# Feed-forward output projections with every matmul split into two 64-row halves

## What is computed

```
def swiglu(h, w_in, w_out):
    g, u = jnp.split(h @ w_in, 2, axis=-1)
    return (jax.nn.silu(g) * u) @ w_out

# in second_block, for each layer
h = modulate(rms_norm(x, norm_g[layer, 0]), sh1, sc1)
x = x + 0.5 * g1[:, None, :] * swiglu(h, ffn_w_in[layer, 0], ffn_w_out[layer, 0])
...
h = modulate(rms_norm(x, norm_g[layer, 2]), sh3, sc3)
x = x + 0.5 * g3[:, None, :] * swiglu(h, ffn_w_in[layer, 1], ffn_w_out[layer, 1])
```

## Time and profile before

| | |
|---|---|
| median of 3 runs | 3966.06 us |
| profiled execution | 3976.6 us, of which the span from first to last instruction is 3974.8 us |
| mean granted TensorE clock | 0.938 |
| PE busy | 3643.8 us, 92% |
| DVE busy | 2207.9 us, 56% |
| ACT busy | 1592.4 us, 40% |
| matmul records | 19924 |

### The profile page before, as it was taken

The page is one execution under the profiler, slowest core; times in us unless marked ns, Lnnn a source line. Parts: engine busy times, 40 slices in busy tenths (PEclk is TensorE's granted clock), DMA queues, the critical chain, the costliest instruction groups (busy, mean ns, idle before and its releaser), DMA issues.

```text
span 3974.8 us, 52209 instructions
## 1 busy us (share of the span) xinstructions
PE 3643.8 (92%) x19924; PEld 2788.9 (70%) x19924; DVE 2207.9 (56%) x3277; ACT 1592.4 (40%) x2692; POOL 303.7 (8%) x401
## 2 busy tenths in 40 slices
PE   8998796998999586998999998999999999889998
PEld 7886475666787454456878766787877878667877
DVE  7866855886874784236772336565233332654332
ACT  3335744887423662113222336322233222453222
POOL 0110001110210002001210000111000001000001
PEclk9999588999999758999999999999999999999999
DMA  7561013997555005997773310575323223302222
GB/s 276 175 172 61 2 59 123 365 362 277 185 191 150 1 33 212 403 395 251 271 251 101 101 64 11 180 232 197 106 82 125 96 96 103 130 33 88 95 93 74
DMA packets 164958, 618.35 MB, mean 156 GB/s; under 512 B 18540, under 2 KB 20117, under 8 KB 163581
## 3 DMA queue, kind: packets, MB, share of 16 engines
q1 hardware_dynamic: 114928, 420.58, 29.7%
q0 software_dynamic: 45568, 166.75, 12.8%
q10 hardware_dynamic: 4238, 27.90, 1.8%
HBM read 595.95 MB, written 16.31 MB: 154 GB/s over the span
## 4 chain that ended last, share of the span: by engine, by line
PE 82%; DVE 8%; ACT 5%; DMA 2%; issue 2%; SPq 0%; ACTq 0%; POOL 0%; DVEq 0%; POOLq 0%; PEldq 0%
PE psum L2500 23%; PE psum L2513 12%; PE psum L838 12%; PE psum L923 5%; PE psum L990 4%; PE psum L2103 4%; PE psum L767 3%; PE psum L2334 3%; PE psum L2122 2%; DMA ring<-wtile 1%; PE psum L2355 1%; PE psum L1207 1%; PE psum L1217 1%; PE psum L775 1%; DVE spare L1313 1%
## 5 line engine op out<-in xcount | busy, mean ns | idle before, releaser
L791 ACT CAST small_r<-ring 128x1024 fp32r<-128x1024 f32 x264 | 276.0, 1048 | 1081.9 <-PE psum L838 336.9
L795 DVE TENSOR_TENSOR ring_r<-ring,small_r 128x1024 fp32r<-128x1024 f32 x264 | 323.7, 1228 | 687.9 <-ACT small_r L791 687.7
L791 ACT CAST PB_r<-ring 128x1024 fp32r<-128x1024 f32 x248 | 257.3, 1049 | 545.8 <-PE psum L2500 327.9
L795 DVE TENSOR_TENSOR ring_r<-ring,PB_r 128x1024 fp32r<-128x1024 f32 x248 | 299.6, 1222 | 247.6 <-ACT PB_r L791 247.2
L2500 PE MATMUL psum<-H_r,ring_r 128*128 128x512 f32 x1344 | 336.1, 392 | 0.0
L2500 PE MATMUL psum<-H_r,small_r 128*128 128x512 f32 x1344 | 326.9, 395 | 0.0
L2500 PE MATMUL psum<-H_r,PB_r 128*128 128x512 f32 x1344 | 318.6, 389 | 0.0
L2500 PEld LDWEIGHTS psum<-H_r,small_r 128*128 128x128 f32 x1344 | 252.3, 188 | 61.2
L2500 PEld LDWEIGHTS psum<-H_r,ring_r 128*128 128x128 f32 x1344 | 252.2, 188 | 56.0
L2500 PEld LDWEIGHTS psum<-H_r,PB_r 128*128 128x128 f32 x1344 | 252.3, 188 | 53.4
L838 PE MATMUL psum<-H_r,small_r 128*128 128x512 f32 (+1 forms) x1040 | 275.4, 368 | 0.0
(11 more groups left out here) (443 smaller groups left out, 6615.5 us busy)
## 6 DMA issues: line engine op xcount, KB each, us to landing
ring<-wtile SPq DMA_DIRECT2D x776, 512.0 KB, 5.1
spare<-wmod POOLq DMA_DIRECT2D x97, 512.0 KB, 4.8
H<-wmod POOLq DMA_DIRECT2D x48, 512.0 KB, 4.6
PB<-wmod POOLq DMA_DIRECT2D x48, 512.0 KB, 4.4
X<-wmod POOLq DMA_DIRECT2D x47, 512.0 KB, 5.1
PB<-wahead POOLq DMA_DIRECT2D x16, 512.0 KB, 7.7
h_rows<-PB POOLq DMA_DIRECT2D x10, 512.0 KB, 4.5
PB<-wmod SPq DMA_DIRECT2D x4, 1024.0 KB, 15.2
```

The source lines that it names most:

```text
L791: nc.scalar.copy(high(j), slot(g0 + j)).then_inc(high_ready.sem, 1)
L795: nc.vector.tensor_tensor(low(g0 + j), slot(g0 + j), high(j).bitcast(F32), ALU.subtract).then_inc(low_ready.sem, 1)
```

## The change

Each matmul of the output phase is made as two. The first contracts partitions 0 to 63 of the weight tile and of the hidden, into bank 4 or 5 as before. The second contracts partitions 64 to 127, into bank 6 or 7. Both have 128 output rows and 512 columns. `out(j)` adds the two banks to `X` one after the other; the second addition waits for the first, since it reads what that wrote.

```
+            ROW_HALVES = (slice(0, P // 2), slice(P // 2, P))
...
-                                    mm = nc.tensor.matmul(bank[4 + j % 2][:, :], w_part[:, k * P:(k + 1) * P], HID2[x][:, kk * NLAT:(kk + 1) * NLAT],
-                                                          start=(not last and kk == 0 and x == 0), stop=(last and kk == FT - 1))
+                                    for h, r in enumerate(ROW_HALVES):
+                                        mm = nc.tensor.matmul(bank[4 + j % 2 + 2 * h][:, :], w_part[r, k * P:(k + 1) * P], HID2[x][r, kk * NLAT:(kk + 1) * NLAT],
+                                                              start=(not last and kk == 0 and x == 0), stop=(last and kk == FT - 1))
...
-                    nc.vector.scalar_tensor_tensor(Xv[:, j, 0:NLAT], bank[4 + j % 2][:, :], coef[:, 16 + j:17 + j], Xv[:, j, 0:NLAT],
+                    V(eng, nc.vector.scalar_tensor_tensor(Xv[:, j, 0:NLAT], bank[4 + j % 2][:, :], coef[:, 16 + j:17 + j], Xv[:, j, 0:NLAT], ALU.mult, ALU.add))
+                    nc.vector.scalar_tensor_tensor(Xv[:, j, 0:NLAT], bank[6 + j % 2][:, :], coef[:, 16 + j:17 + j], Xv[:, j, 0:NLAT],
                                                    ALU.mult, ALU.add).then_inc(dve_freed.sem, 1)
```

## The result

The changed kernel takes 3977.43 us (median of 20 runs, 3963.78 to 3992.29) beside 3964.60 us for the kernel before (20 runs, 3952.99 to 3971.49). The ratio is 1.0028, with a 95% interval of 1.0019 to 1.0037. It is slower by some 11 us (0.0028 x 3965), more than the 4.8 us forecast, inside the stated range and beyond the 0.2% that the prediction took as the limit of no change, though the interval just reaches down to it. The mean granted clock over the 20 runs of the changed kernel is 0.9380.

The account below looks back on a forecast made before the run. TensorE was taken as the bound, with 82% of the chain of waits. 1.6 us of offsets and 3.2 us of additions, with nothing for the clock, made +4.8 us on 3966.06, about 3971 us; range 3952 to 3990.

Parts of the forecast that it names:

- The likeliest case: Whole kernel: pairs as fast as single matmuls, 3958 to 3974 us, no change beyond 7.9 us; chance 0.50.
- a cost kept by each pair: Output-phase matmuls: each pair costs 1.5 to 12 ns more than a whole matmul, so slower; chance 0.28.
- Pairs run together: Output phase on TensorE: two 64-row matmuls run at the same time, taking as long as one 128-row matmul.
- 1.6 us for an offset once per wait: Output phase: 7 to 10 ns at each of 192 waits, two per weight tile, +1.6 us.
- The bounds of -30 and +21 us: Output-phase pairs: limits from halves winning 14 ns per pair to an extra 10 ns per pair.
- 3.2 us for four additions on the chain: End of each output phase: the last tile's second addition adds 0.79 us, four times, +3.2 us; the 28 others hidden.
- Nothing for the clock, with 5 us either way: After the longer idle behind three phases: granted clock loss taken as unchanged, bounded by 3 x 1.7 = 5 us.
- The first rival: Output-phase matmuls: each pair keeps a cost, 7 ns or 14.8 us, giving 3984 us; chance 0.28 for 1.5 to 12 ns.
- the second, faster halves: Output-phase matmuls: halves escape a slowdown in reading by 8 ns, 17 us less, giving 3954 us; chance 0.08.
- Serial halves: Output-phase matmuls: fp32r halves do not overlap, 0.230 us each, +486 us, 4455 us; chance 0.08.
- Exposed loads: Output phase: each weight load waits for the matmul before it on the same rows, +397 us, 4366 us; chance 0.06.

Follow-up runs that it names:

- same_rows: The changed kernel with both matmuls of a pair on rows 0 to 63, same counts, banks and additions: 5297.76 us.
- halves_only: The changed kernel's half matmuls in two banks, but one addition, of the first bank only: 3962.35 us, 1.0001 of the kernel before.
- again: The changed kernel run once more, unaltered: 3974.11 us, 1.0019 of the kernel before.
- adds_only: The kernel before with whole matmuls, but each addition doubled, the same bank added twice at half the scale: 3974.13 us, 1.0020 of the kernel before.
- one_half: The changed kernel with only the first half of each matmul, rows 0 to 63, and one addition: 4378.23 us.
- last_whole: The changed kernel with the last output tile of each feed-forward in whole matmuls and one addition: 3970.68 us, 1.0018 of the kernel before.
- four_adds: The kernel before with whole matmuls, but four chained additions of the same bank at a quarter of the scale: 3985.9 us, 1.0058 of the kernel before.
- the filled kernels: The kernel before and the changed one, each with three unused matmuls in the wait after the first three feed-forwards: 3960.7 us (0.9989) and 3961.3 us (0.9999).

## Why the prediction was right, and where it was off

The forecast was 3971 us and the time 3977.4, in the range of 3952 to 3990. The likeliest case, no change beyond 7.9 us, did not come by the ratio of 1.0028, which lies just outside it, on the side that had 0.42. That side was meant for a cost kept by each pair, which is not there, so that the time came slower and inside the range is in part luck: the room made for such a cost took in a loss of clock that was put at nothing.

- **Pairs run together.** Right, and shown by `same_rows` and `halves_only`. The row that carried it was the fp32 score product, four records in 1.13 us beside two in 1.12; it held for fp32r in a stream of 2112 pairs.
- **1.6 us for an offset once per wait.** Too much: the steady 24 pairs take 5.59 us in both traces, and `halves_only` has 492.2 us of phases as before. The starts of a pair were to be a few ns apart; they are 3 to 37 ns apart, and it costs nothing. The bounds of -30 and +21 us were not needed. The first rival, a cost of each pair, is refuted at this pace, and so is the second, faster halves.
- **3.2 us for four additions on the chain.** Right in each place: 6.09 to 6.88 us at three and 2.43 to 3.21 at the last. In the traces the 28 others hold nothing up.
- **Nothing for the clock, with 5 us either way.** This is the mis-sized term. The runs put 6 to 7 us on it, by a mean clock of 0.9385 in place of 0.9409, all of it a loss and beyond the bound of 5, and it comes with the additions and not with the halves. The prediction counted the stretch right behind the idle, where the first pairs of `again` and `adds_only` are no longer than those of profiles with the short wait. How the remaining microseconds spread over later stretches was not found; one profile per kernel is too few, since stages that are not changed differ by as much from profile to profile (from the end of the third first pair to the fourth input phase before took 211.4 us and `halves_only` 206.4).
- **The rivals' prices.** Serial halves were priced at +486 us, at the full clock. The run that made them serial lost 1308 us in the phases, at a granted clock of 0.50. Exposed loads did not come; the trace of `one_half` has them covered on the same rows.

Still open: the 5.6 us of `last_whole`, which stretches hold the loss of clock, and with it whether the added idle causes that loss or only goes with it. For a cause speak `four_adds` and the filled kernels, against it the table of waits and `last_whole`.

## What to carry to other kernels

Two matmuls on different row halves, into different banks and near each other in the queue, take the time of one, so a split by contraction rows neither costs nor gains on TensorE; what it costs is the second bank's addition where that stands behind the last matmul. Do not price such a step by its length on the chain alone: here 3.2 us on the chain came to about 10. Where TensorE waits for a chain of other engines, a few matmuls without use can keep the clock: with three of them the first pair took 7.49 us at all six places, 1.6 less than the usual 9.05. The gain for the whole kernel, 4 us by the means, is not clear of the noise.

## What the runs showed of the hardware

- A stream of fp32r matmuls of rows 0 to 63 alone ran at a granted clock of 0.50 with PE busy all the time, 0.426 us for 512 columns; two such streams on different rows ran at 1.00, 0.230 us a pair. Half the array in use took nearly twice the time of all of it.
- Matmuls on free rows start ahead of earlier ones that wait for theirs, over a limited reach: 175.4 us a phase where full overlap gives 122.9.
- Four matmuls of 32 rows and their four loads fit in 0.230 us.
- The loss of clock behind an idle TensorE was 1.6 us of a first pair of 9.05 (7.49 where it was filled, and once without); from profile to profile the same wait of 6.09 us was followed by 7.49 to 9.97 us.
- With the wait stretched to 9.4 us by three additions, the clock fell inside it, and the two records of a sum took 2.08 in place of 1.14 us.
- The two halves of a pair started 3 to 37 ns apart, steady within a phase, without any effect on the step of 0.230 us. Between 64-row and 128-row matmuls two steps were 0.32 and 0.34 us long.
